# High and low parts of a weight stream: the low part over the landed weights, four buffers, splits of 1024 columns

## What is computed

```python
def mixer_sublayer(h, w_in, b_forget, ...):            # layer 1
    proj = h @ w_in                                    # 2048 x 7176
    ...
    return merged @ w_out                              # 2048 x 2048

def peer_sublayer(h, w_query, sub_keys, u, v):         # layer 1, experts
    q = (hb @ w_query).reshape(PEER_BLOCK, PEER_HEADS, 2, D_KEY // 2)
    s = jnp.einsum('thpc,hpnc->thpn', q, sub_keys).astype(jnp.float32)
    top_s, top_i = lax.top_k(s, PEER_TOPK)             # top 16 of 128, then of the 256 sums
    ...
    g = jax.nn.softmax(best_s, axis=-1)
    a = jax.nn.gelu(jnp.einsum('thkd,td->thk', u_sel, hb), approximate=False)
    return jnp.einsum('thk,thkd->td', (g * a).astype(hb.dtype), v_sel)
...
# layer 2: h @ w_in_2, w_glu, w_attn_br, w_ssm_br, w_out_2, w_up (5632 x 2), w_down
```

## Time and profile before

| what | value |
|---|---|
| time, median of 3 runs | 4381.94 us (4374.06 to 4382.52) |
| profiled execution | 4374.01 us, of it span 4372.4 us |
| PE busy | 3801.7 us, 87% of the span |
| DVE busy | 2794.1 us, 64% |
| ACT busy | 2065.8 us, 47% |
| POOL busy | 173.5 us, 4% |
| read from memory | 714.89 MB, 164 GB/s over the span |

### The profile page before, as it was taken

The page is one execution under the profiler, slowest core; times in us unless marked ns, Lnnn a source line. Parts: engine busy times, 40 slices in busy tenths (PEclk is TensorE's granted clock), DMA queues, the critical chain, the costliest instruction groups (busy, mean ns, idle before and its releaser), DMA issues.

```text
span 4372.4 us, 79572 instructions
## 1 busy us (share of the span) xinstructions
PE 3801.7 (87%) x26598; PEld 3516.3 (80%) x26598; DVE 2794.1 (64%) x4758; ACT 2065.8 (47%) x3408; POOL 173.5 (4%) x210
## 2 busy tenths in 40 slices
PE   7997678899999996899999969994336879999998
PEld 6997448799999995788888769993116879999998
DVE  5776525478874449755555567775796656666555
ACT  3443514466664440255555534551443336666554
POOL 1000000000000004100000000000120000000000
PEclk9998759899999997899999989995668989999999
DMA  6993004445555550255555558860002435555554
GB/s 251 347 346 106 0 12 164 147 160 180 174 182 184 185 184 12 96 188 187 187 188 188 189 193 331 336 243 0 10 10 93 144 119 183 183 183 185 172 184 158
DMA packets 184040, 719.87 MB, mean 165 GB/s; under 512 B 20528, under 2 KB 23088, under 8 KB 171056
## 3 DMA queue, kind: packets, MB, share of 16 engines
q1 hardware_dynamic: 166464, 608.57, 39.9%
q0 software_dynamic: 14592, 102.77, 6.5%
q10 hardware_dynamic: 2928, 7.83, 0.5%
HBM read 714.89 MB, written 4.19 MB: 164 GB/s over the span
## 4 chain that ended last, share of the span: by engine, by line
PE 79%; DVE 14%; issue 3%; ACT 2%; DVEq 1%; DMA 0%; ACTq 0%; POOL 0%; POOLq 0%
PE PS L398 19%; PE PS L400 19%; PE PS L399 19%; PE PS L477 5%; PE PS L476 5%; PE PS L478 5%; DVE arena L1303 2%; PE PS L393 1%; DVE big L1053 1%; PE PS L531 1%; DVE arena L1115 1%; PE PS L501 1%; DVE big L1070 1%; DVE big L1310 1%; DVE arena L1070 1%
## 5 line engine op out<-in xcount | busy, mean ns | idle before, releaser
L1010 DVE TENSOR_TENSOR wlo<-raw,whi 128x512 fp32r<-128x512 f32 x2300 | 1557.5, 690 | 1187.3 <-ACT whi L742 1174.9
L742 ACT ACTIVATE whi<-raw 128x512 fp32r<-128x512 f32 x2300 | 1438.2, 631 | 1529.2 <-PE PS L400 1169.8
L398 PE MATMUL PS<-hhi,whi 128*128 128x256 f32 (+1 forms) x7168 | 2031.6, 283 | 126.1 <-DVE hlo L1023 111.7
L399 PE MATMUL PS<-hlo,whi 128*128 128x256 f32 (+1 forms) x7168 | 2029.7, 283 | 0.0
L400 PE MATMUL PS<-hhi,wlo 128*128 128x256 f32 (+1 forms) x7168 | 2028.9, 283 | 0.0
L398 PEld LDWEIGHTS PS<-hhi,whi 128*128 128x128 f32 x7168 | 1361.1, 190 | 137.6 <-issue 115.7
L400 PEld LDWEIGHTS PS<-hhi,wlo 128*128 128x128 f32 x7168 | 1362.6, 190 | 0.0
L399 PEld LDWEIGHTS PS<-hlo,whi 128*128 128x128 f32 x7168 | 1355.1, 189 | 0.0
L476 PE MATMUL PS<-whi,hhi 128*128 128x512 f32 x1024 | 403.5, 394 | 1.8 <-issue 1.8
L477 PE MATMUL PS<-wlo,hhi 128*128 128x512 f32 x1024 | 403.8, 394 | 0.0
L478 PE MATMUL PS<-whi,hlo 128*128 128x512 f32 x1024 | 403.6, 394 | 0.0
(11 more groups left out here) (356 smaller groups left out, 2392.0 us busy)
## 6 DMA issues: line engine op xcount, KB each, us to landing
raw<-peer_u_dram SPq DMA_DIRECT2D x256, 512.0 KB, 3.3
raw<-peer_v_dram SPq DMA_DIRECT2D x256, 512.0 KB, 3.2
raw<-w_in_dram SPq DMA_DIRECT2D x240, 512.0 KB, 4.7
big<-w_mod_dram POOLq DMA_DIRECT2D x96, 1024.0 KB, 5.0
raw<-w_up_dram SPq DMA_DIRECT2D x176, 512.0 KB, 3.3
raw<-w_down_dram SPq DMA_DIRECT2D x88, 512.0 KB, 3.2
raw<-w_out_dram SPq DMA_DIRECT2D x64, 512.0 KB, 3.3
raw<-w_query_dram SPq DMA_DIRECT2D x32, 512.0 KB, 3.2
```

The costliest lines, as they stand in the source:

```text
L398: pe.matmul(out, hi, rhi, start=start, stop=False, **more)
L399: pe.matmul(out, hi, rlo, start=False, stop=False, **more)
L742: f(whi[:, m % PAIRS, quarter(q)], raw[:, m % RING, quarter(q)], ACT.Copy).then_inc(hi_ready, 1)
L1010: dv.tensor_tensor(wlo[:, m % PAIRS, quarter(q)], raw[:, m % RING, quarter(q)], whi[:, m % PAIRS, quarter(q)], ALU.subtract).then_inc(lo_r ...
```

## The change

- `wlo` has no memory of its own any more. It lies at the same address as `raw`, four buffers, and DVE's subtract writes the low part over the landed weights that it reads. `whi` has four buffers in place of two. `PAIRS` is gone: PE, ACT and DVE take buffer m % 4 of all three.
- A half is copied and subtracted in one instruction of 1024 columns on each engine. Both add 2 to their semaphore at its end. The copy waits on no quarter of PE any more, only on the load.
- SP's load of half m waits on `quarters_used`, until PE has used half m - 4 whole.
- Waits of the take-outs count from `RING` in place of `PAIRS`, which names the same point of PE's work.

```diff
+        at_raw = -(-nc.sbuf_base // 32) * 32
         raw = sb("raw", [P, RING, HALF])
-        whi = sb("whi", [P, PAIRS, HALF], F32R)
-        wlo = sb("wlo", [P, PAIRS, HALF], F32R)
+        wlo = nc.alloc_sbuf_tensor_at("wlo", [P, RING, HALF], F32R, offset=at_raw)
+        whi = sb("whi", [P, RING, HALF], F32R)
...
-                        sp.wait_ge(lo_ready, g * (2 * RING) + 2 * (FIRST[name] + s + 1))
+                        sp.wait_ge(quarters_used, g * (2 * RING) + 2 * (FIRST[name] + s + 1))
                         sp.dma_start(raw[:, s, :], d[name][g * RING + s]).then_inc(raw_in[s], 16)
...
-                                last = three(PS[:, c, 0:width], whi[:, half, at_], wlo[:, half, at_],
+                                s_ = (2 * c + half) % RING
+                                last = three(PS[:, c, 0:width], whi[:, s_, at_], wlo[:, s_, at_],
...
                     sc.wait_ge(raw_in[m % RING], g * 32 + 16 * (m // RING + 1))
-                    for q in range(2):
-
-                        sc.wait_ge(quarters_used, g * 16 + (2 * m + q + 1))
-                        f(whi[:, m % PAIRS, quarter(q)], raw[:, m % RING, quarter(q)], ACT.Copy).then_inc(hi_ready, 1)
+                    f(whi[:, m % RING, :], raw[:, m % RING, :], ACT.Copy).then_inc(hi_ready, 2)
...
-                        sc.wait_ge(quarters_used, g * 16 + 2 * (PAIRS + FIRST[name] + 2 * (at + k + 1)))
+                        sc.wait_ge(quarters_used, g * 16 + 2 * (RING + FIRST[name] + 2 * (at + k + 1)))
...
-                    for q in range(2):
-                        dv.wait_ge(hi_ready, g * 16 + (2 * m + q + 1))
-                        dv.tensor_tensor(wlo[:, m % PAIRS, quarter(q)], raw[:, m % RING, quarter(q)],
-                                         whi[:, m % PAIRS, quarter(q)], ALU.subtract).then_inc(lo_ready, 1)
+                    dv.wait_ge(hi_ready, g * 16 + (2 * m + 2))
+                    dv.tensor_tensor(wlo[:, m % RING, :], raw[:, m % RING, :], whi[:, m % RING, :],
+                                     ALU.subtract).then_inc(lo_ready, 2)
...
-            dv.memset(gmod[:, 15:16], 0.0).then_inc(quarters_used, 2 * PAIRS)
+            dv.memset(gmod[:, 15:16], 0.0).then_inc(quarters_used, 2 * RING)
```

More of the change, by code:

```diff
@@ L431, in dense_half @@
                             at_ = slice(kc * P, (kc + 1) * P)
-                            last = three(PS[:, c % 4, 0:SEQ], whi[:, c % 2, at_], wlo[:, c % 2, at_],
+                            last = three(PS[:, c % 4, 0:SEQ], whi[:, c % RING, at_], wlo[:, c % RING, at_],
                                          hhi[:, base + kc, META:], hlo[:, base + kc, META:], kc == 0, kc == 7)
@@ L449, in body @@
                                 at_ = slice(m * P, (m + 1) * P)
-                                last = three(PS[:, mm // 2, (mm % 2) * SEQ:(mm % 2 + 1) * SEQ], whi[:, half, at_],
-                                             wlo[:, half, at_], hhi[:, b % 2, META:], hlo[:, b % 2, META:],
+                                s_ = (2 * b + half) % RING
+                                last = three(PS[:, mm // 2, (mm % 2) * SEQ:(mm % 2 + 1) * SEQ], whi[:, s_, at_],
+                                             wlo[:, s_, at_], hhi[:, b % 2, META:], hlo[:, b % 2, META:],
                                              opening and b == 0 and mm % 2 == 0, False, skip_group_check=True)
@@ L475, in body @@
                                     bank = PS[:, t * 4 + half * 2 + q, :]
-                                    pe.matmul(bank, hhi[:, b % 2, o_], whi[:, half, quarter(q)], start=opens, stop=False, skip_group_check=True)
-                                    pe.matmul(bank, hhi[:, b % 2, o_], wlo[:, half, quarter(q)], start=False, stop=False, skip_group_check=True)
-                                    last = pe.matmul(bank, hlo[:, b % 2, o_], whi[:, half, quarter(q)], start=False,
+                                    pe.matmul(bank, hhi[:, b % 2, o_], whi[:, s_, quarter(q)], start=opens, stop=False, skip_group_check=True)
+                                    pe.matmul(bank, hhi[:, b % 2, o_], wlo[:, s_, quarter(q)], start=False, stop=False, skip_group_check=True)
+                                    last = pe.matmul(bank, hlo[:, b % 2, o_], whi[:, s_, quarter(q)], start=False,
                                                      stop=False, skip_group_check=True)
@@ L871, in gelus @@
                 split(g, FIRST["peer_u"] + 2 * start, 2 * k + 2)
-                sc.wait_ge(quarters_used, g * 16 + 2 * (PAIRS + FIRST["peer_u"] + 2 * (start + k + 1)))
+                sc.wait_ge(quarters_used, g * 16 + 2 * (RING + FIRST["peer_u"] + 2 * (start + k + 1)))
                 f(ga[:, g * 4 + (start + k), :], PS[:, k, 0:SEQ], ACT.Gelu).then_inc(banks_free, 1)
@@ L962, in _ @@
                     split(0, FIRST["w_glu"], k + 2)
-                sc.wait_ge(quarters_used, 2 * (PAIRS + FIRST["w_glu"] + k + 1))
+                sc.wait_ge(quarters_used, 2 * (RING + FIRST["w_glu"] + k + 1))
                 f(glug[:, k, :], PS[:, k % 4, 0:SEQ], ACT.Sigmoid,
@@ L1296, in _ @@
             dv.wait_ge(banks_free, 4 + 216)
-            dv.wait_ge(quarters_used, 2 * (PAIRS + FIRST["peer_v"]))
+            dv.wait_ge(quarters_used, 2 * (RING + FIRST["peer_v"]))
             dv.memset(small[:, 26:27], 0.0).then_inc(gates_used, 4)
@@ L1327, in _ @@
             for q in range(4):
-                dv.wait_ge(quarters_used, 2 * (PAIRS + FIRST["w_in_2"]) - 3 + q)
+                dv.wait_ge(quarters_used, 2 * (RING + FIRST["w_in_2"]) - 3 + q)
                 move(acc_t[:, 1, q * 512:(q + 1) * 512], PS[:, 4 + q, :]).then_inc(acc_copied, 1)
```

20 lines of the change are left out of this document (9 added, 11 removed).

## The result

| what | before | after |
|---|---|---|
| time, median (lowest to highest) | 4379.51 us (4374.06 to 4382.52), 4 runs | 4433.49 us (4428.73 to 4445.78), 4 runs |
| profiled execution, its span | 4374.01, 4372.4 us | 4428.73, 4427.1 us |

The ratio is 1.0133, with a 95% interval of 1.0118 to 1.0148: the changed kernel is slower by 54 us. The prediction said 4370 (4352 to 4390). It was wrong, and on the wrong side. Two single runs at a much lower mean granted clock, 4704.87 us (0.772) in experiment 3 and 12017.11 us (0.422) in experiment 8, are in the medians given there and not in the ratios.

A forecast was written before the change was run, and what follows sets the result against it. TensorE was taken as the bound, 79% of the span, with the splits following it. Terms -9.3 - 8 + 5.7 + 4 = -7.6 us gave 4366 on the profiled execution and 4374 on the median; the middle, 4370, was forecast, range 4352 to 4390.

The forecast's parts named there:

- w_mod's stages: w_in and w_in_2: a few bursts of slow landings over 5.4 us (6.1 in w_in) stop PE, +4 us, bounds 0 and +27.
- rival A: w_in and w_in_2: loads come late and stop every tile, +27 us in place of +4, time 4393; chance 0.12.
- the chain through the accumulate: w_in and w_in_2: next first half ready at landing + 6.0, behind DVE's 2.35 us accumulate; landings over 5.4 (6.1) stop PE.
- the shorter chain: Plain stages, second half of a pair: ready at t + 5.86, due at t + 8.52, slack 2.7 us, so loads stay hidden.
- Which load waits: w_in_2: w_mod's load keeps its 5.0 us and the raw load waits; under even sharing, 4 us less.
- w_up: w_up, after each silu: the first split has 1024 columns, PE starts 0.26 later, 22 times, +5.7 us, bounds +2 and +9.
- peer_u with the top 16: First half of peer_u, with the selection: PE's gaps shrink by 0.5 in 16 rounds, -8 us, bounds 0 and -15.
- the smaller gaps of the other three tiles: peer_u's selection stretch: gaps of 0.25 us a round close, as copies no longer wait for quarters; part of the -8.
- rival B: peer_u gains nothing, since DVE's blocks are the chain there: 4378 us; chance 0.14.
- Ends of stages: Stage ends: the last pair is split earlier, 1.13 us in five stages, 0.54 in five, 0.9 after w_glu; -9.3 us in all.
- The subtract over its own input: DVE's subtract of 1024 columns written over the weights it reads: taken at the same 1.22 us.
- The plain stages: w_out, w_query, peer_v, w_down: loads stay hidden with 2.7 us slack and PE shows no new wait.

The follow-up runs named there:

- experiment 3: The changed kernel with copies and subtracts of 512 columns (quarters) again, four buffers kept: 4383.15 us, ratio 1.0011 to the kernel before.
- experiment 8: Control: the kernel before with only the w_mod loads moved to SyncE's queue: 4379.39 us, ratio 0.9999 to the kernel before.
- experiment 1: The kernel before with only the load's wait moved from DVE's subtract to PE's last use, two buffers and quarters kept: 4407.76 us, ratio 1.0073.
- experiments 4 to 6: Changed kernel: w_mod loads in SP's queue (4), 4401.66 us; nearly no w_mod traffic (5), 4368.97 us; as 4, w_in_2's w_mod loads one place later (6), 4382.47 us.
- experiment 7: The changed kernel with splits of 512 columns and the w_mod loads in SyncE's queue behind the raw loads: 4354.11 us, ratio 0.9952 to the kernel before.
- experiment 5: The changed kernel with each w_mod load moving only 16 of 2048 columns: 4368.97 us in one run, beside 4381.99 for the kernel before.
- experiment 2: The kernel before with only copy and subtract merged to 1024 columns, in two buffers: 4564.05 us, ratio 1.0431.

## Why the prediction was wrong, point by point

- **w_mod's stages, the step that failed.** "I expect 4 to 5.4 and no stop in most tiles", worth +4, was +56.0. The prediction's rival A had the mechanism, late loads, but not its size. Three things were wrong. First, "the raw load is issued 0.7 later against the tile" is 4.3 by the rows above; I had looked at the order within one tile and not at which half a load writes over. So nothing of the old cover was left. Second, and by the count of second halves the larger part, the landings were taken as given, and they grew: landings as before would have gone over the slack by 5.1 us in w_in_2 and never in w_in, and in after they did by 24.2 and 21.6. w_mod's median went from 5.0 to 6.3 in w_in_2 and to 7.6 in w_in, and raw loads over 8 us from 2 to 6 in w_in_2. The argument "PE that stops asks for less, and a landing then shortens" did not hold. Third, the price was put on the chain through the accumulate (5.4), while most stops came by the shorter chain that I had kept for the plain stages ("gone only when a landing takes over 5.9 us"), and the clock behind a long stop was not in the sum. I had read the median and the maximum of a piece of the stage, and neither tells how many lie over a threshold. The terms 1.14 and 2.26 of that chain stand in no row; in after it is 1.15 and 2.26 from one start on DVE to the next (2703.60, 2704.75, 2707.01), so the sum of 6.0 stands. The prediction's A was priced at +27, half of what came; experiments 1 and 3 show +31 and +27 for the late request with quarters, and whole halves add the other 29. A quarter as first piece gives back 1.22 - 0.69 + 1.05 - 0.63 = 0.95 us, so the slack of 5.96 would be some 6.9 there (an estimate): two parts of the change spend the same slack. Why the landings grow when the request comes late stays open; experiments 4 to 6 show that it takes w_mod's loads, and that their place in the stream decides.
- **Which load waits.** The prediction held that w_mod's load keeps its time and the raw load waits for it. In after both took 8.2 to 8.8. This is nearer to the rule of the Trainium skill (DMA: Bandwidth & Descriptors, "Queues, rings and completion order") that each DMA engine takes turns between the rings. What I made of that rule, a raw load slowed by at most 1.3 us, was wrong, since it counted one pair of loads, and at 2712.7 two raw loads and two of w_mod were under way.
- **w_up**, +5.7 forecast, +13.5 measured. The mechanism is right: 21 waits of PE behind the subtract in the stretch shown, 11.1 us, or 0.53 each. The size is off: from the take-out to PE's start I had 3808.69 - 3802.88 = 5.81, and it took 3857.27 - 3851.25 = 6.02. Of the 0.21, 0.13 lie between the take-out and the copies (3.58 for 3.45), 0.07 between copy and subtract (1.16 for 1.09): hand overs that I had counted at nothing or 0.05. So a round is late by 0.47 and not 0.26, which makes 10.3 us in 22 rounds; I can't place the other 3. Experiments 3 and 7 (-3.3 and -3.4) show that the loss is all of the whole halves'.
- **peer_u with the top 16**, -8 forecast; peer_u and peer_v together gained 4.4 and the gaps of PE stayed (6.8 of 349 us). The prediction's rival B (peer_u gains nothing) was nearer. The step that failed is "the smaller gaps of the other three tiles [...] should close". There were none: in both traces PE stops once in a round, behind the long block, for 0.45 us before and 0.4 to 0.5 in after (15 stops, 6.7 us, and 14 stops, 6.8 us, from 920 to 1269). From a take-out to the one four tiles on it is 23.68 us before, 23.57 in after and 22.9 in experiment 3, where four tiles without a stop take 22.72. So the time was there to gain, -12.8 with quarters and a PE without gaps, and the merged subtract takes it back: behind the long block it ends 0.53 later (1.22 for 0.69). That had been counted (1051.2 to 1052.4); what the earlier start of the block gives was put too high.
- **Ends of stages**, -9.3 forecast. w_out's end gained 0.89 for 1.13. The rows of the table without w_mod, selection or silu (w_out and w_query, s5 and w_glu to w_out_2, w_down) sum to -8.8, and 1.5 went back between peer_v and w_in_2: -7.3 net. But of the ends in the forecast these rows hold only some, worth 6.0 (4 x 1.13 + 0.54 + 0.9); the others lie in rows where other effects are mixed in, and the 1.3 of w_down was not forecast. The direction and the size of one end are shown, the total of -9.3 is not.
- **The subtract over its own input**: 1224 ns against 1219. Right.
- **The plain stages**: w_out, w_query, peer_v and w_down showed no new wait, landings 3.3. Right.
- **Attention** has the same code in all kernels and took 265.3 to 278.7 us. The time follows the granted clock, which is 0.65 to 0.69 there: PE works little and the clock is at its lower level for 164 to 195 us of the stage. The row of the kernel before, and the same stretch of experiment 8 and of experiment 5:

```profile
390.00:662.20 272.20, 175.92 (x592) 124.47 (x592) 133.03 (x192) 93.37 (x137) 3.95 (x2) 0.66 0.04 14
388.50:667.10 278.60, 182.01 (x592) 126.98 (x592) 132.96 (x192) 93.27 (x136) 3.95 (x2) 0.65 0.04 14
388.40:653.70 265.30, 166.79 (x592) 118.85 (x592) 132.66 (x192) 93.24 (x136) 3.95 (x2) 0.69 0.04 15
```

The same 592 matmuls keep PE busy for 175.9, 182.0 and 166.8 us. It shifts single executions by some 7 us in either direction, and fits the two groups, near 4373 and 4381 us, into which the runs of the kernel before fall (mean clock 0.915 and 0.912). In after it is -3.1, in experiment 7 -1.0, so no verdict here rests on it. In experiment 1 it is +6.1 of the 39 in the profiled execution, in experiment 5 -6.8.

## What to carry to other kernels

If a change moves the gate of a load from an early consumer to a late one, follow one buffer through a whole turn of the ring to get the new slack, and count the landings that exceed it, not their median; do so for each half of a tile with its own chain, and expect the landings to grow, too. Where two streams of loads share the DMA engines, try them in one queue in the order of need: here it gave back 51 of the 56 us, and 20 of these hung on the place. And merging two instructions into one saved nothing here, since both engines wait, while it delayed the first piece by 0.95 us: do it only where nobody waits for that piece.

## What the runs showed of the hardware that I had not expected

- With a 1 MB load of POOL's queue and 512 KB loads of SP's queue under way together, landings reached 8.8 and 8.4 us, where w_mod's fastest took 4.9 and the raw loads without w_mod 3.3. The DMA engines were busy for 0.94 of that time, at 360 GB/s, and for 0.21 right behind the stop: bursts and lulls in place of an even stream. In one queue (experiment 7) w_mod takes 6.1 and the raw loads 4.3 in the median, at most 7.7, at 326 GB/s, and PE is busy for 339.02 of 340 us. What part the queue has in this and what part the place was not settled.
- A stop of TensorE can cost more than its length. Behind stops of 2.00 to 3.04 us (w_in_2 in after) and of 2.03 us (19 of 21 in w_up in experiment 2) the granted clock was 0.50 for 3.4 us, with 16 to 19 matmuls for 31. PE's idle time understates such stops: 18.5 us idle in the stretch for 32.2 us lost.
